# Two heads of a class side by side on the array, one accumulator, and attention work moved between the chunks of the query/key/value projection

## The chip, the cores and the metric

The kernel runs on one core of one Trainium2 chip. The metric is the device time of one execution in microseconds (us), and the median of several executions is what counts. Everything is 32-bit; weights and activations of the large products are split into a high and a low part, so that one product is three matrix multiplications.

## The reference

One inference step of a two-layer decoder trunk, for a prompt of 512 tokens and 8 sample tokens that share the weights: layer 0 is a gated short convolution, layer 1 a dilated sliding-window attention, and each is followed by a gated ConvFFN. The change is in layer 1:

```python
GROUPS = ((128, 1), (512, 4), (2048, 16))        # window, dilation; 8 heads of 64 in each group
q, k = rmsnorm(p[..., 0]), rmsnorm(p[..., 1])    # per head, p = h @ w_qkv
logits = einsum('bqhd,bqkhd->bqhk', q, kg) * SCALE + bias     # kg: the keys at dilated distances
out, lse = softmax(logits) @ vg, m + log(s)
w = softmax(stack(lses)); out = sum(w[g] * outs[g])           # merge of the three groups
mp = op @ attn_w_out                                          # and the same for the sample tokens, with caches
```

## The kernel before

The five engines run programs written out by hand, one block each (`block.sync`, `block.scalar`, `block.vector`, `block.tensor`, `block.gpsimd`), and meet at semaphores. The order of the code is the order of the work. All weights pass through the same pipeline of **chunks** of 1024 x 128 weights: SP loads a chunk into one of four slots (`load`), ScalarE copies its high part (`split_hi`, L711), VectorE subtracts for the low part (`split_lo`, L1016), and TensorE multiplies (`products`, L1508). A chunk is 8 k-steps of 6 matmuls each with 260 columns, 48 in all. Its result lands in one of two accumulators `acc[:, 0]` and `acc[:, 1]`, taken in turn (`cc % 2`).

The attention layer is the stage `S_QKV` of 36 chunks: four passes p = 0 to 3, one for each pair of heads, with nine chunks c = 0 to 8 (query, key, value of three groups). VectorE reads each result (`tile_out`), ScalarE squares it, TensorE sums over a head (`head_sums`, L1711), ScalarE makes the inverse root (`head_rms`), VectorE multiplies (`normalise`, L1306), and keys and values are transposed (`kv_transpose`).

The attention of pair p-1 runs among the chunks of pass p. Queries fall into four classes (position mod 4), and the softmax of one head and one class is a **unit**; a pair of heads has eight. All three groups are merged in a single softmax over 768 logits. A unit is: `unit_logits` (L1679 with 512 columns, L1680 and L1681 with 128, contraction over the 64 rows of one head), `unit_softmax` on VectorE (L1246, L1250, then L1256, L1257) around `exp_unit` on ScalarE (L876), `unit_transpose` (L1497, six of them), copies out of PSUM (`pt_copy` L882 on ScalarE, `unit_pt` L1230 on VectorE), `unit_values` (L1699, L1700, L1703) and `unit_o` (L1238). TensorE does all of that at one place, before k-step 3 of a chunk: `products(..., {3: at})`. Once in a pass, at c = 8, `sample_values` (L1778) multiplies the cached values of the eight sample tokens: 24 products of two columns, in one run.

After chunk 35 the last pair's attention runs among the eight small chunks (three k-steps, 18 matmuls) of the output projection `S_WO` (`part_products`, `part_residual`). Then come the last k-step of that projection (L1883) and the second ConvFFN. I call the stretch from the end of chunk 35 to L1883 the **stage end**.

In the trace, 32-bit matmuls of attention appear as two instructions (two **passes**); L1508 and transposes appear as one.

Of the kernel before, what the change touches and what calls it, by code (L numbers as in the profile page):

```python
# [143 lines left out]
def build(nc, x_prompt, x_sample, state_sc, cache1, cache4, cache16, state_ffn, norm_mix, norm_ffn, sc_w_in,  # L144
# [10 lines left out]
    with ExitStack() as ctx:  # L155
# [32 lines left out]
        small = sb("small", [P, 8])  # L188
# [23 lines left out]
        inv = attn(2 * TT).rearrange("p (t n) -> p t n", t=2)  # L212
        v_t = attn(2 * SEQ).rearrange("p (t n) -> p t n", t=2)
# [3 lines left out]
        lg = attn(6 * P)  # L217
        pr = attn(6 * P)
# [62 lines left out]
        softmax_steps = sem("softmax_steps")  # L281
        neg_ready = sem("neg_ready")
        e_ready = sem("e_ready")
        p_ready = sem("p_ready")
        pt_ready = sem("pt_ready")
        pt_act = sem("pt_act")
        pt_dve = sem("pt_dve")
        o_ready = sem("o_ready")
        o_kept = sem("o_kept")
        kt_ready = sem("kt_ready")  # L290
        vt_ready = sem("vt_ready")
        kt_kept = sem("kt_kept")
        vt_kept = sem("vt_kept")
# [71 lines left out]
        PT = (lg[:, 0:4 * P], lg[:, 4 * P:6 * P])  # L365
        PT_LAST = (held[:, 0:4 * P], held[:, 4 * P:6 * P])
# [8 lines left out]
        def logit_parts(bank):  # L375
            return (bank[0:W, 0, HALF:HALF + P], bank[0:W, 1, HALF:HALF + P], bank[0:W, 1, HALF + P:HALF + P + SK[2]])
# [29 lines left out]
        def _(sp):  # L406
# [102 lines left out]
            def pair_rows_out(p):  # L509

                sp.wait_ge(vt_kept, 3 * p + 3)
                sp.wait_ge(kt_kept, 3 * p + 3)
# [19 lines left out]
            def sample_loads(ps, c):  # L532

                if c == 0:
                    if ps:
                        sp.wait_ge(samp_v, ps)
                    cache_rows(ps, 0, 0, skv[:, 0], skv_in[0])
                    sp.wait_ge(rowq_out, 16 * (ps + 1))
                    query_rows(ps, 0, skv[:, 1], skv_in[1])
                    cache_rows(ps, 1, 0, skv[:, 2], skv_in[2])  # L540
                    rows_to_dram(ps)
                elif c == 1:
                    pair_rows_out(ps)
                    sp.wait_ge(samp_prod, 3 * ps + 1)
                    query_rows(ps, 1, skv[:, 1], skv_in[1])
                elif c == 2:
# [3 lines left out]
                    fresh_rows(ps, 0, skv[:, 0], skv_in[0])  # L550
                    sp.wait_ge(samp_prod, 3 * ps + 2)
                    query_rows(ps, 2, skv[:, 1], skv_in[1])
                elif c == 3:
# [4 lines left out]
                elif c == 4:  # L558
# [6 lines left out]
            for cc in range(9 * NP_):  # L565
# [11 lines left out]
                if c == 8:  # L577
# [7 lines left out]
                    query_rows_to_dram(p)  # L585
# [5 lines left out]
            cache_rows(ps, 0, 0, skey(ps, 0), skv_in[0])  # L591
            sp.wait_ge(rowq_out, 16 * (ps + 1))
            query_rows(ps, 0, squery(ps, 0), skv_in[1])
            cache_rows(ps, 1, 0, skey(ps, 1), skv_in[2])
# [102 lines left out]
        def _(act):  # L697
# [241 lines left out]
            for cc in range(9 * NP_):  # L939
# [9 lines left out]
                if p and c < 8:  # L949
                    exp_unit(n0 + c)  # L950
# [998 lines left out]
```

## Time and profile before

| | us |
|---|---|
| median of 3 runs | 1432.86 (1432.2 to 1434.42) |
| the profiled execution, its own time | 1435.17 |
| its span, first to last instruction | 1433.5 |
| TensorE matmul busy | 1398.5 (98%) |
| VectorE busy | 766.1 (53%) |
| ScalarE busy | 506.3 (35%) |
| mean granted TensorE clock | 0.982 |

### The profile page before, as it was taken

How to read it: one execution, taken by the hardware profiler on the slowest of the kernel's cores; microseconds unless marked ns; L12 is line 12 of the kernel's file. 1: busy time of each engine (PE TensorE's matmuls, PEld its weight loads, DVE VectorE, ACT ScalarE, POOL GpSimd, SP SyncE). 2: the span in 40 equal slices, each digit the busy share in tenths (PEclk: the TensorE clock that was granted, in tenths of full speed). 3: DMA queues.
4: the chain of work that ended last, by engine and by line, in shares of the span. 5: the costliest groups of instructions: out<-in, count | busy, mean ns of one | idle time of the engine just before them, and what ended most of it. 6: DMA issues, size and time to landing. Idle time of an engine off the chain costs nothing.

```text
span 1433.5 us, 27779 instructions
## 1 busy us (share of the span) xinstructions
PE 1398.5 (98%) x11153; PEld 1353.7 (94%) x11153; DVE 766.1 (53%) x1250; ACT 506.3 (35%) x811; POOL 21.1 (1%) x50
## 2 busy tenths in 40 slices
PE   6999999999999999999999999989899999999998
PEld 5999999999999999999899899887799999999998
DVE  4655566556555433445655646647576565553222
ACT  4322234343333332334334333423353344332112
POOL 0000000000000000000000000000000000000000
PEclk9999999999999999999999999988799999999999
DMA  6354435654444444547526317337224454455331
GB/s 169 89 167 134 142 111 190 188 162 121 148 136 147 140 134 132 161 124 217 151 68 204 109 63 209 95 99 207 89 74 128 139 172 117 127 157 165 109 89 64
DMA packets 256586, 195.17 MB, mean 136 GB/s; under 512 B 6581, under 2 KB 250789, under 8 KB 255362
## 3 DMA queue, kind: packets, MB, share of 16 engines
q1 hardware_dynamic: 253528, 139.17, 34.3%
q0 software_dynamic: 1792, 54.43, 10.7%
q8 instruction: 53, 0.87, 0.3%
q10 hardware_dynamic: 1194, 0.54, 0.1%
q14 instruction: 19, 0.16, 0.0%
HBM read 186.60 MB, written 65.21 MB: 176 GB/s over the span
## 4 chain that ended last, share of the span: by engine, by line
PE 93%; DVE 3%; issue 1%; DMA 1%; ACT 1%; SPq 0%; DVEq 0%
PE acc L1508 78%; PE N L1497 3%; PE M L1679 2%; PE acc L1536 2%; PE acc L1778 2%; PE N L1711 2%; PE M L1703 1%; PE M L1699 1%; DMA wraw<-in_sc_w_in_dram 1%; PE M L1681 0%; PE M L1680 0%; DMA skv<-new_rows 0%; PE M L1536 0%; PE M L1700 0%; DVE wl L1016 0%
## 5 line engine op out<-in xcount | busy, mean ns | idle before, releaser
L1508 PE MATMUL acc<-hh,wh 128*128 128x260 f32 x2288 | 468.8, 286 | 0.9 <-DVE wl L1016 0.9
L1508 PE MATMUL acc<-hh,wl 128*128 128x260 f32 x2288 | 463.1, 284 | 0.0
L1508 PE MATMUL acc<-hl,wh 128*128 128x260 f32 x2288 | 462.7, 284 | 0.0
L711 ACT ACTIVATE wh<-wraw 128x1024 fp32r<-128x1024 f32 (+1 forms) x212 | 220.7, 1041 | 551.1 <-PE acc L1508 539.3
L1508 PEld LDWEIGHTS acc<-hh,wh 128*128 128x128 f32 x2288 | 356.7, 190 | 3.0 <-issue 1.1
L1508 PEld LDWEIGHTS acc<-hh,wl 128*128 128x128 f32 x2288 | 355.2, 190 | 0.0
L1508 PEld LDWEIGHTS acc<-hl,wh 128*128 128x128 f32 x2288 | 354.7, 190 | 0.0
L1016 DVE TENSOR_TENSOR wl<-wraw,wh 128x1024 fp32r<-128x1024 f32 (+1 forms) x212 | 254.3, 1199 | 176.7 <-ACT wh L711 171.1
L1508 PE MATMUL acc<-yh,wh 128*128 128x260 f32 x848 | 173.1, 285 | 0.0
L1508 PE MATMUL acc<-yh,wl 128*128 128x260 f32 x848 | 171.5, 284 | 0.0
L1508 PE MATMUL acc<-yl,wh 128*128 128x260 f32 x848 | 171.4, 284 | 0.0
L1508 PEld LDWEIGHTS acc<-yh,wh 128*128 128x128 f32 x848 | 131.4, 189 | 0.9 <-issue 0.4
L1508 PEld LDWEIGHTS acc<-yl,wh 128*128 128x128 f32 x848 | 132.0, 190 | 0.0
L1508 PEld LDWEIGHTS acc<-yh,wl 128*128 128x128 f32 x848 | 131.6, 190 | 0.0
L1180 DVE TENSOR_TENSOR u<-acc,r 128x512 f32<-128x512 f32 x44 | 30.4, 692 | 120.3 <-PE acc L1508 119.1
L876 ACT ACTIVATE big<-big,small 128x768 f32<-128x768 f32 x32 | 30.1, 939 | 106.9 <-DVE small L1250 106.9
L1497 PE MATMUL N<-ident,big 128*128 128x128 f32 (+4 forms) x307 | 43.2, 279 | 12.7 <-DVE big L1257 7.6
L810 ACT ACTIVATE sv<-cv 128x536 f32<-128x536 f32 x44 | 28.7, 652 | 73.6 <-DVE cv L1059 73.6
L1050 DVE TENSOR_TENSOR x<-acc,x 128x520 f32<-128x520 f32 (+1 forms) x24 | 16.8, 700 | 64.6 <-PE acc L1508 61.9
L1497 PEld LDWEIGHTS N<-ident,big 128*128 128x128 f32 (+4 forms) x307 | 35.4, 146 | 14.3 <-issue 12.7
L1188 DVE TENSOR_TENSOR t<-sv,r 128x512 f32<-128x512 f32 x44 | 30.5, 692 | 31.6 <-ACT sv L810 31.6
L1057 DVE SCALAR_TENSOR_TENSOR cv<-u,params,cv 128x536 f32<-128x536 f32 x52 | 40.4, 777 | 11.2 <-ACT cv L750 7.5
(205 smaller groups left out, 1194.9 us busy)
## 6 DMA issues: line engine op xcount, KB each, us to landing
out_dram<-in_cache_kv_d_dram POOLq DMA_DIRECT2D x24, 1364.0 KB, 6.3
wraw<-in_ffn_w_gate_dram SPq DMA_DIRECT2D x44, 512.0 KB, 3.8
wraw<-in_ffn_w_up_dram SPq DMA_DIRECT2D x44, 512.0 KB, 3.9
wraw<-in_attn_w_qkv_dram SPq DMA_DIRECT2D x36, 512.0 KB, 3.9
out_dram<-in_cache_kv_d_dram POOLq DMA_DIRECT2D x8, 2044.0 KB, 8.3
wraw<-in_ffn_w_down_dram SPq DMA_DIRECT2D x32, 448.0 KB, 3.7
wraw<-in_sc_w_in_dram SPq DMA_DIRECT2D x24, 512.0 KB, 3.9
wraw<-in_ffn_w_down_dram SPq DMA_DIRECT2D x16, 512.0 KB, 4.0
```

The source lines that it names most:

```text
L711: nc.scalar.activation(wh[c % 2][:, 0:k], wraw[:, c % 4, 0:k], ACT.Copy).then_inc(hi_done, 1)
L810: nc.scalar.activation(sv[:], cv[:], ACT.Silu).then_inc(silu_ready, 1)
L876: nc.scalar.activation(pr[:], lg[:], ACT.Exp, bias=small[:, 1:2], scale=-1.0, accum_out=small[:, 2:3]).then_inc(e_ready, 1)
L1016: V.tensor_tensor(wl[c % 2][:, 0:k], wraw[:, c % 4, 0:k], wh[c % 2][:, 0:k].bitcast(F32), ALU.subtract).then_inc(split_done, 1)
L1057: ch.after(V.scalar_tensor_tensor(out=cv[:], in0=u[:, 1:1 + CO], scalar=params[:, bass.ds(f + w1, 1)], in1=cv[:], op0=ALU.mult, op1=ALU.add))
L1180: V.tensor_tensor(u_prompt, acc[:, 0, :, 0:HP], prompt(r), ALU.mult)
L1188: V.tensor_tensor(prompt(t1), conv_prompt(sv), prompt(r), ALU.mult)
L1497: return T.transpose(out, in_, ident[0:k, 0:k])
L1508: ins = T.matmul(acc[:, par, h2, 0:HALF], w[c % 2][:, k, :], a[:, k0 + k, h2, :], start=(first and k == 0 and n == 0), stop=(last and k == ...
L1536: ins = T.matmul(dst[:, h2, 0:HALF], w[c % 2][:, k, :], a[:, k, h2, :], start=(first and n == 0), stop=(last and n == 2))
L1679: T.matmul(M[:, 0, :], k[s, 0, cq], k[s, 1, :], start=True, stop=True)
L1711: ins = T.matmul(N[:, h2, 0:HALF], head_ones[:], sq[:, h2, :], start=True, stop=True)
```

## The change

- **Units.** Both heads of a class are one unit now: four units a pair, 16 in all instead of 32. `unit_logits` takes head 0 on array rows 0 to 63 and head 1 on rows 64 to 127 in turn, with their results in separate PSUM banks; `unit_values` takes them on array columns 0 to 63 and 64 to 127 in turn. The number of matmuls per head is as before.
- **Places.** TensorE does nothing of the prompt's attention inside a chunk. Before an odd chunk c = 1, 3, 5, 7 stand the logits of a unit, with the values of the unit before between their two parts; before an even chunk 2, 4, 6, 8 stand its twelve transposes. `head_sums` and `kv_transpose` come one chunk later than before.
- **One accumulator.** From chunk 9 on all results go to `acc[:, 0]`, so a chunk may start only when `tile_out` has read the one before it. The banks `B0` and `B1` of `acc[:, 1]` hold logits, transposes and outputs of attention.
- **Softmax.** VectorE takes both heads' maxima in a row (`unit_max`), then scales head 0 (`unit_scale`); ScalarE scales head 1 (`scale_unit`) and makes all three copies after the transposes (`pt_copies`). `kv_transpose` results are copied by ScalarE alone.
- **Sample tokens.** `sample_values` is cut into eight pieces of three products, before k-steps 4 to 7 of chunk 8 and 0 to 3 of the next chunk. In SP's queue the sample loads of a pass move by up to a chunk, and `query_rows_to_dram` stands behind the wait on `samp_v`.
- **Stage end.** Four units with two small chunks each; all small chunks use `acc[:, 0]`.

```diff
+        def par(cc):
+            return cc % 2 if cc < 9 else 0
-        PT = (lg[:, 0:4 * P], lg[:, 4 * P:6 * P])
+        B0, B1 = acc[:, 1, 0], acc[:, 1, 1]
+        OUT = slice(2 * P, 3 * P)
...
             def unit_logits(n, between=None):
+                k, cls = qka[:, (n // NCLS) % 2], n % NCLS
+                heads = (slice(0, DH), slice(DH, P))
                 if n:
-                    pe.wait_ge(neg_ready, n)
-                T.matmul(M[:, 0, :], k[s, 0, cq], k[s, 1, :], start=True, stop=True)
-                T.matmul(M[:, 1, 0:P], k[s, 2, cq], k[s, 3, cq], start=True, stop=True)
-                T.matmul(M[:, 1, P:2 * P], k[s, 4, cq], k[s, 5, cq], start=True, stop=True).then_inc(s_ready, 1)
+                    pe.wait_ge(pt_kept, 3 * n)
+                for h2, s in enumerate(heads):
+                    ins = T.matmul(M[:, h2, :], k[s, 0, cq], k[s, 1, :], start=True, stop=True)
+                ins.then_inc(s_ready, 1)
+                if between:
+                    between()
+                for i in (1, 2):
+                    for h2, s in enumerate(heads):
+                        ins = T.matmul((B0, B1)[h2][:, (i - 1) * P:i * P], k[s, 2 * i, cq], k[s, 2 * i + 1, cq],
+                                       start=True, stop=True)
+                ins.then_inc(s_ready, 1)
...
             def unit_values(n, bank):
+                for i in (1, 2):
+                    for h2, s in enumerate(heads):
+                        T.matmul(bank[s, OUT], v[:, i, cls, s], pt_g12[:, (2 * h2 + i - 1) * P:(2 * h2 + i) * P],
+                                 start=(i == 1), stop=False)
                 for t in range(4):
                     lo, hi = 32 * t, min(32 * t + 64, P)
+                    for h2, s in enumerate(heads):
+                        ins = T.matmul(bank[s, OUT][:, lo:hi], v[:, 0, t, s], pt_g0[h2][:, t * P + lo:t * P + hi],
+                                       start=False, stop=(t == 3))
...
+            def pt_copies(n, bank):                          # ScalarE
+                act.wait_ge(pt_ready, 2 * n + 1)
+                nc.scalar.activation(pt_g0[0], bank[:, 0, :], ACT.Copy).then_inc(pt_kept, 1)
+                act.wait_ge(pt_ready, 2 * n + 2)
+                nc.scalar.activation(pt_g12, B1, ACT.Copy).then_inc(pt_kept, 1)
+                nc.scalar.activation(pt_g0[1], bank[:, 1, :], ACT.Copy).then_inc(pt_kept, 1)
...
-                products(S_QKV, 0, cc, cc % 2, DK, hh, hl, 0, True, True, first_chunk(2) if cc == 0 else {3: at})
+                elif p and c == 8:
+                    inserts = {k: (lambda b=k - 4, ps=p - 1: sample_values(ps, B0, b, b + 1)) for k in range(4, 8)}
+                elif p >= 2 and c == 0:
+                    inserts = {k: (lambda b=k + 4, ps=p - 2: sample_values(ps, B0, b, b + 1)) for k in range(4)}
+                free_acc(S_QKV, 0, cc, 2 if cc < 9 else 1)
+                products(S_QKV, 0, cc, par(cc), DK, hh, hl, 0, True, True, inserts)
...
+            for j in range(NCLS):                            # VectorE, stage end
+                unit_max(n, 0)
+                unit_max(n, 1)
+                if j == 3:
+                    sample_norm(p)
+                part_residual(2 * j)
+                unit_scale(n)
+                unit_inv(n)
+                splits(S_WO, 0, 2 * j)
...
+                part_residual(2 * j + 1)
+                splits(S_WO, 0, 2 * j + 1)
+                if j < 3:
+                    key_products(p, j)
+                    key_sums(p, j)
+                if j == 2:
+                    sample_max(p, N[:, 0])
```

On TensorE, in a pass p > 0 of the kernel before, this stands in the middle of a chunk between its third and fourth k-step: transposes of one unit, logits of the next, values of the first, head sums.

```order
L1508 MATMUL acc<-hh,wl 128x260 x2
L1497 MATMUL N<-ident,big 128x128 [waits p_ready,inv_ready]
L1497 MATMUL N<-ident,big 128x128 x5
L1679 MATMUL M<-big 128x512 [waits neg_ready]
L1680 MATMUL M<-big 128x128
L1681 MATMUL M<-big 128x128
L1699 MATMUL M<-big 64x128 [waits pt_dve,pt_act,o_kept]
L1700 MATMUL M<-big 64x128
L1703 MATMUL M<-big 64x64 x3
L1703 MATMUL M<-big 64x32
L1711 MATMUL N<-sv,head_ones 128x260 [waits qsq_ready]
```

In the kernel after, the same engine between an even chunk and the odd one behind it (L1701 and L1709 are the two parts of the logits of both heads, L1736 and L1741 the values of the unit before, L1749 the head sums; `newh_tok` and `big` hold the copied transposes):

```order
L1529 MATMUL acc<-hh,wl 128x260 x2
L1701 MATMUL M<-big 128x512 [waits pt_kept]
L1701 MATMUL M<-big 128x512
L1736 MATMUL acc<-newh_tok,big 64x128 [waits pt_kept]
L1736 MATMUL acc<-newh_tok,big 64x128 x3
L1741 MATMUL acc<-big 64x64 x6
L1741 MATMUL acc<-big 64x32 x2
L1709 MATMUL acc<-big 128x128 x4
L1749 MATMUL N<-sv,head_ones 128x260 [waits qsq_ready,inv_ready]
L1749 MATMUL N<-sv,head_ones 128x260
L1529 MATMUL acc<-hh,wh 128x260 [waits split_done,acc_free]
```

What was four changes of operation for one head is four for two heads now, the two heads alternate in each row, and the wait for the accumulator stands behind all of it.

On TensorE in chunk 8 of a pass, after the change, the sample tokens' values stand between k-steps, three products at a time (L1813):

```order
L1529 MATMUL acc<-hh,wl 128x260 x2
L1813 MATMUL acc<-cv,skv 128x2 x3
L1529 MATMUL acc<-hh,wh 128x260 x2
L1529 MATMUL acc<-hl,wh 128x260 x2
L1529 MATMUL acc<-hh,wl 128x260 x2
L1813 MATMUL acc<-cv,skv 128x2 x3
```

Before, L1778 stood there once with all 24 products in one row.

On VectorE, before the change, one unit stands in one chunk, and the reading of the chunk's result behind it (L1246 and L1250 the maxima, L1256 and L1257 the scaling, L1271 and L1273 the result's reading, L1016 the split):

```order
L1246 ISA big,small<-M,big 128x512 [waits s_ready]
L1246 ISA small 128x1
L1250 ISA big,small<-M,big,small 128x256 [waits dve_chain]
L1250 ISA small 128x1
L1356 RECIPROCAL small<-small 16x1 [waits samp_e]
L1357 TENSOR_SCALAR cv<-cv,small 16x323 [waits dve_chain]
L1256 RECIPROCAL small<-small 128x1 [waits e_ready]
L1257 TENSOR_SCALAR big<-big,small 128x768 [waits dve_chain]
```

After it, in an odd chunk, both heads' maxima stand in a row (L1252, L1256), then the split (L1030), `unit_o` (L1245) and the scaling of head 0 (L1263, L1264); the reading of the last chunk's result (L1283, L1285) stands ahead of them:

```order
L1252 ISA big,small<-M,big 128x512 [waits dve_chain,s_ready]
L1252 ISA small 128x1
L1256 ISA big,small<-acc,big,small 128x256 [waits s_ready,dve_chain]
L1256 ISA small 128x1
L1252 ISA big,small<-M,big 128x512 [waits s_ready]
L1252 ISA small 128x1
L1256 ISA big,small<-acc,big,small 128x256 [waits s_ready,dve_chain]
L1256 ISA small 128x1
L1030 TENSOR_TENSOR wl<-wraw,wh 128x1024 [waits hi_done]
L1245 COPY t<-acc 128x128 [waits o_ready]
L1263 RECIPROCAL small<-small 128x1 [waits e_ready]
L1264 TENSOR_SCALAR big<-big,small 128x768 [waits dve_chain]
```

The reading of the result moved ahead of the softmax, and the scaling of head 1 is no longer VectorE's.

## Rows read from the trace of the kernel before

**Rows 1.** The page: busy time, and the chain's shares by engine.

```profile
PE 1398.5 (98%) x11153; PEld 1353.7 (94%) x11153; DVE 766.1 (53%) x1250; ACT 506.3 (35%) x811; POOL 21.1 (1%) x50
PE 93%; DVE 3%; issue 1%; DMA 1%; ACT 1%; SPq 0%; DVEq 0%
```

**Rows 2.** Windows of passes 1 and 3 and the stage end: busy us, clock.

```profile
core 0: us, PE busy (x) PEld busy (x) DVE busy (x) ACT busy (x) POOL busy (x), PEclk, DMA share, GB/s
662.13:760.78 98.65, 97.92 (x744) 88.78 (x743) 57.57 (x124) 37.09 (x61) 0.49 (x1) 0.97 0.45 134
...
859.39:958.04 98.65, 97.92 (x744) 88.79 (x742) 56.73 (x124) 36.01 (x61) 0.99 (x2) 0.97 0.41 121
955.85:1030.95 75.10, 64.14 (x415) 54.50 (x413) 44.32 (x102) 21.86 (x41) 0.98 (x2) 0.84 0.61 174
```

**Rows 3.** TensorE's timeline, one insertion of pass 1: start us, us.

```profile
710.51 0.82 PE L1497 MATMUL N<-ident,big 128*128 128x128 f32 x6
711.26 1.12 PE L1679 MATMUL M<-big 64*128 64x512 f32 x2
712.22 0.38 PE L1680 MATMUL M<-big 64*128 64x128 f32 x2
712.44 0.38 PE L1681 MATMUL M<-big 64*128 64x128 f32 x2
712.75 0.43 PE L1699 MATMUL M<-big 128*64 128x128 f32 x2
713.02 0.38 PE L1700 MATMUL M<-big 128*64 128x128 f32 x2
713.25 0.60 PE L1703 MATMUL M<-big 128*64 128x64 f32 x8
713.77 1.14 PE L1711 MATMUL N<-sv,head_ones 128*128 128x260 f32 x4
```

**Rows 4.** Timeline of TensorE's weight loads, an insertion ten us earlier.

```profile
702.33 0.30 PEld L1681 LDWEIGHTS M<-big 64*128 64x128 f32 x2
...
703.14 0.59 PEld L1703 LDWEIGHTS M<-big 128*64 128x64 f32 x8
```

**Rows 5.** TensorE's timeline at c = 8 of pass 1.

```profile
744.45 0.40 PE L1699 MATMUL M<-big 128*64 128x128 f32 x2 [0.73 <-ACT big L882]
...
746.54 6.61 PE L1778 MATMUL acc<-cv,skv 128*128 128x2 f32 x48
```

**Rows 6.** Windows of L1778 alone (two), then of L1508 alone (two).

```profile
746.54:750.44 3.90, 3.90 (x36) 3.90 (x36) 1.00 0.50 196
750.44:753.01 2.57, 2.57 (x14) 2.57 (x13) 0.51 0.00 0
...
753.01:757.30 4.29, 4.29 (x20) 4.29 (x21) 0.50 0.01 4
757.30:760.78 3.48, 3.48 (x30) 3.43 (x29) 0.99 0.00 0
```

**Rows 7.** TensorE's waits from 958 to 1031 us: total, times, longest.

```profile
PE N L1497 <- DVE big L1257: 7.6, 6, 4.3
PE acc L1778 <- DVE cv L1364: 2.5, 1, 2.5
```

**Rows 8.** Timelines of VectorE and ScalarE, one chunk of pass 1.

```profile
704.11 0.67 DVE L1246 CUSTOM_DVE_ANT_0 big<-M,big 128x512 f32<-128x512 f32 x1
704.98 0.49 DVE L1250 CUSTOM_DVE_ANT_0 big<-M,big,small 128x256 f32<-128x256 f32 x1 [0.19 <-DVE small L1246]
...
706.77 0.62 DVE L1257 TENSOR_SCALAR big<-big,small 128x768 f32<-128x768 f32 x1
...
709.93 1.22 DVE L1016 TENSOR_TENSOR wl<-wraw,wh 128x1024 fp32r<-128x1024 f32 x1 [0.25 <-DVE big L1273]
...
705.51 0.94 ACT L876 ACTIVATE big<-big,small 128x768 f32<-128x768 f32 x1 [3.55 <-DVE small L1250]
```

**Rows 9.** SP's timeline in pass 2, and DMA issues from 660 to 860 us (KB each, us to landing).

```profile
770.08 6.35 SPq L515 DMA_DIRECT2D out_dram<-big  x1
...
skv<-in_cache_kv_d_dram SPq DMA_DIRECT2D x8, 512.0 KB, 5.5
```

More of the change, by code:

```diff
@@ new lines, in _ @@
+                if c in SUMS and p >= SUMS[c][0]:
+                    head_rms(6 * (p - SUMS[c][0]) + SUMS[c][1])
+                if c % 3:
+                    squares(6 * p + 2 * (c // 3) + c % 3 - 1)
+                if p >= 2 and c == 0:
+                    pair_y(p - 2)
+                    sample_y(p - 2, B0)
+            p, n0 = NP_ - 1, (NP_ - 1) * NCLS
+            step(S_QKV, 0, 9 * NP_ - 1)
+            head_rms(6 * NP_ - 1)
+            keep_queries(p, M[:, 0])
+            pair_y(p - 1)
@@ new lines, in _ @@
+                if p >= 2 and c == 0:
+                    unit_o((p - 1) * NCLS - 1, B1)
+                    pair_y(p - 2)
+                if c in SUMS and p >= SUMS[c][0]:
+                    normalise(p - SUMS[c][0], SUMS[c][1])
+                if p and c == 1:
+                    key_products(p - 1, 0)
+                if p and c == 2:
+                    key_sums(p - 1, 0)
+                    key_products(p - 1, 1)
+                if p and c == 4:
+                    key_sums(p - 1, 1)
+                    key_products(p - 1, 2)
+                    key_sums(p - 1, 2)
@@ L1419, in part_residual @@
+                if p and c == 6:
+                    sample_max(p - 1, B0)
+                if p and c == 7:
+                    sample_norm(p - 1)
+                if p and c == 8:
+                    sample_pts(p - 1, B0)
+                if p >= 2 and c == 0:
+                    sample_y(p - 2, B0)
             def part_residual(m):
@@ L1747, in sample_logits @@
                 pe.wait_ge(samp_lt, 3 * ps + 3)
-                for g, part in enumerate(logit_parts(bank)):
+                for g in range(NG):
+                    part = bank[0:W, SCOL[g]:SCOL[g] + SK[g]]
                     n = NBACK[g] + (1 if g == 2 else 0)
@@ L1818, in _ @@
-                free_acc(S_QKV, 0, cc)
+                n = (p - 1) * NCLS + (c - 1) // 2
+                if c in ROWS and p >= ROWS[c][0]:
+                    n_read(p, c)
+                    kv_transpose(p - ROWS[c][0], ROWS[c][1])
+                if p and c % 2:
+                    if c == 1 and p >= 2:
+                        pe.wait_ge(ys_lo, p - 1)
+                    if c == 1:
+                        pe.wait_ge(tb_in, 16 * p)
+                        pe.wait_ge(rowq_kept, p)
+                    if c == 7:
+                        pe.wait_ge(samp_m, p)
+                    if c == 1:
+                        unit_logits(n, lambda p=p: row_transpose(p - 1))
+                    else:
+                        unit_logits(n, lambda n=n: unit_values(n - 1, B1))
@@ L1868, in _ @@
-            sample_values(p, acc[:, 1], 4, 6)
-            unit_values(n0 + 7, N, PT_LAST)
-            sample_values(p, acc[:, 1], 6, NS)
+            part_products(1)
+            pe.wait_ge(kv_kept, 3 * NP_)
+            for j in range(NCLS):
+                if j == 3:
+                    pe.wait_ge(samp_m, NP_)
+                unit_transpose(n0 + j, N)
+                if j < 3:
+                    unit_logits(n0 + j + 1)
+                    part_products(2 * j + 2)
+                    unit_values(n0 + j, N[:, 1])
+                    if j == 2:
+                        sample_logits(p, N[:, 0])
+                    part_products(2 * j + 3)
```

493 lines of the change are left out of this document (206 added, 287 removed).

## The prediction

> **What bounds the kernel now.** First the page: TensorE is busy for 98% of the span and is 93% of the chain that ended last, while VectorE is busy for 53% [rows 1]. So a saving on TensorE is a saving of time, and one on VectorE is not. The questions are what TensorE does in the attention layer, and where it waits or runs slowly. The windows answer both [rows 2]: the passes 1 to 3 (three of them, first and last shown) take 98.65 us each with TensorE busy for 97.9, VectorE for 57. The stage end takes 75.10 with TensorE busy for 64.1, so it is a chain of waits there. The granted clock is 0.97 in a pass and 0.84 in the stage end.
>
> The timeline of one insertion [rows 3] gives the price of a head's unit: transposes 710.51 to 711.26, 0.75; logits to 712.75, 1.49; values to 713.77, 1.02. That is 3.26 us for each of 32 units, none of it waiting. The timeline at c = 8 shows a stall of 0.73 before the values and then the sample tokens' run of 48 passes, 746.54 to 753.01, 6.47 us [rows 5]. The windows of that run alone [rows 6] say more: 36 passes in 3.90 us at a clock of 1.00, so 0.108 each, then 0.51, the 1.2 GHz level; and the 20 matmuls of the chunk behind it took 0.215 each at 0.50, where 30 took 0.116 each at 0.99. TensorE fell to the low level in the middle of a run of two-column products and stayed there for some 6.8 us.
>
> **What the change saves on TensorE.** (a) *Sample values between k-steps.* 48 passes by 0.108 are 5.2 against 6.47: 1.27. The 20 slow matmuls cost 20 x (0.215 - 0.116) = 1.98. Both passes shown have the same clock and length, so I take three such places: 9.7. In 24 pieces there is an edge each; I allow 0.05 for one, 1.2. Left: 8.5. It assumes that the clock stays at 1.00 when half of the time between pieces is 260-column work (three products, 0.65, then a k-step, 0.7).
>
> (b) *The 0.73 stall* [rows 5]: the values waited for ScalarE's copy right behind the transposes. After the change a chunk lies between. Three times: 2.2.
>
> (c) *Fewer changes of operation.* Six transposes take 0.75 where five spacings of 0.108 and a pass would be 0.65; L1681 holds TensorE for 0.31 before L1699, where L1680 took 0.22 [rows 3]. So a change of shape costs about 0.1. Before there are four a head, eight a class, after it five a class: 0.3 by 16 classes, 4.8. Matmuls and columns are otherwise the same. The Trainium skill (TensorEngine Tiling, Key Properties) says that a change of tiling mode drains the engine, which speaks against putting the values between the two parts of the logits; the trace has the drain at about 0.1 us, and by it the count of changes still falls.
>
> (d) *Two heads on two halves.* The trace of before has no two matmuls on different halves next to each other, so I bound it. Each product is two passes, and the second of a head must follow its first. In the row head 0, 0, head 1, 1 only neighbours of different heads can run together: four 512-column passes take three slots, eight 128-column passes five. Lowest: nothing, 0. Highest: logits' first part, one slot of 0.48 (0.96 for two passes, L1679); second part, three of 0.11, 0.33; values' 128-column passes, 0.33; the short ones, 0.53 a head for eight, seven of 16 slots of 0.066, 0.46 [rows 3]. That is 1.60 a class, 25.6 in all. Between them: the weight loads. Two loads of 128 columns of weights come 0.11 apart, (0.30 less one load of 0.19), and eight of 64 columns 0.065 apart [rows 4], which is as long as the passes that they feed. If loads go on one after another, then the second part of the logits and the short values gain nothing, the 512-column passes gain their 0.48 and the values' 128-column passes (loads of 64 columns) 0.33: 0.81 a class, 13.0 us. I take this one: it is in the middle, and the rows show TensorE's short passes spaced as their loads are.
>
> **What it costs.** (e) *One accumulator.* `free_acc` now waits for the read of the chunk just ended: 0.68 and 0.15 on VectorE and a hand-over, about 1.1 after the last matmul. Between chunks TensorE has at least 12 transposes and head sums, 1.3 + 0.8; that hides it. Only before chunk 9 there are head sums alone and VectorE reads a value tile: 0.7 once. (f) *The softmax of two heads in one chunk.* Counted from the end of the logits: maxima of two heads 2.0 (0.49 + 0.67 + 0.49 and the gaps of 0.2 between) [rows 8], split 1.2, `unit_o` 0.4, reciprocal and scaling 0.8, the other reciprocal 0.2, ScalarE's scaling 0.9: 5.5. The chunk takes 5.8 and head 0's transposes 0.65 more. It fits by 0.9, so 0. VectorE's 57 us per pass [rows 2] fit too in some 90. (g) *SP's queue.* The cache and query loads now wait for sample products in the middle of the next pass's first chunk, some 5 us into it, and the small query rows go out behind a 512 KB load that takes 5.5 to land; SP itself is held for 6.35 by one row-out DMA [rows 9]. Queued behind the waiting SP are the second query broadcast and the weights; the weights have four chunks to spare. VectorE's `key_products` of c = 2 I reckon late by 2 to 4 us, and behind it stand the next `tile_out` and maxima; TensorE's 4 us of work before chunk 3 cover most. I allow 1 a pass, 3.
>
> (h) *Stage end.* Before: waits of 7.6 and 2.5 for VectorE [rows 7] and 0.9 before L1883. After, in order: TensorE waits for `ys_lo`, since ScalarE copies the 1024 columns of `kv_transpose` before `sample_y`, about 2.0; the second small chunk waits for the first one's `part_residual`, which stands behind four maxima, 0.9; each `unit_logits` now follows its transposes directly and waits for ScalarE's three copies, 3 x 1.4; and at j = 2, `sample_max` waits for `sample_logits`, and behind it on VectorE stand both maxima, `sample_norm` and `part_residual(6)`, for which the seventh small chunk waits: 1.2 + 2.8 + 0.6 + 0.8, about 5.5. Sum 12.6 against 11.0: a loss of 1.6. Its slow stretches (0.16 of 75.1, 12 us before) I leave as they are: the 4.3 us wait goes, a 5.5 us wait comes. The saving of (c) and (d) there is counted.
>
> Sum: 8.5 + 2.2 + 4.8 + 13.0 - 0.7 - 3.0 - 1.6 = 23.2. The profiled execution took 1435.17, so 1412.0; it lies 2.3 above the median 1432.86, and against that the forecast is **1409.6**.
>
> **The rivals.** *No overlap at all.* The halves run one after another: 13.0 less, 1422.6. For it: passes before were never closer than their own length. Against it: they always used the same rows. *Full overlap*: 12.6 more, 1397.0. For it: loads on different halves read different partitions, and nothing in the rows forbids two at once. The Trainium skill (TensorEngine Tiling, Key Properties) says so: different tiles can load weights and multiply in parallel; no row here shows two at once. *The clock falls all the same* in the cut-up sample values: half of their time is two-column work. Then (a) keeps nothing of 1.27 + 1.98 at three places, 9.7 back: 1419.3. For it: the fall came after 3.9 us of such work [rows 6]; against it: insertions of 3 to 4 us with fp32 work at full width never brought it [rows 2, 3]. *Slower than before*: the two-head softmax does not fit into a chunk, and TensorE waits before the transposes at twelve even chunks, with the clock falling where the wait is long. It decides from 23.2 / 12 = 1.9 us a place, so if the chain of (f) is 2.8 longer than reckoned; at 3 us a place the time is 1409.6 + 36 = 1446. VectorE at 57 of 98 us speaks against it, the key products in the same queue for it. *The change does nothing* on balance, because the stage end loses what the passes gain: it would need a stage end of 98 instead of 75 us; 1433.
>
> **How the numbers follow.** Likeliest case 0.48 (alone 1403 to 1417), no overlap 0.22, full overlap 0.13, clock falls 0.10, slower 0.05, nothing 0.02. The range for 8 in 10 runs from 1396 (full overlap) to 1424 (no overlap, and the clock case); what it leaves out is the slow rival, a combination of no overlap with a falling clock or longer waits, and a stage end without slow stretches on top of full overlap. A measurement of this kernel tells about 0.2%, 2.9 us, from no change. Faster by more than that: all cases but the last two and a part of no overlap with the clock falling, 0.92; same 0.03; slower 0.05.
>
> **What would show each step.** In the profile after: the windows of a pass near 90 us and the clock in it 1.00 (a); no stall of 0.7 at L1736 (b); starts of head 1's 512-column passes with or right behind head 0's second, and first parts of logits lasting 1.4 rather than 1.9 (d); TensorE's waits for `acc_free` and p_ready below 1 us a pass (e, f); VectorE's waits for DMA at `key_products` of a few us a pass (g); in the stage end one wait of about 5 us before the seventh small chunk, three of 1.4 before logits, and a stretch near 76 us (h). The prediction is wrong if 512-column passes of two heads stand 0.43 apart throughout, if the clock in c = 8 falls to 0.5, or if TensorE's waits in the three passes come to more than 10 us.

## The result and the profile after

The kernel after takes **1395.2 us** (median of 4, 1393.51 to 1396.47), against 1432.53 (median of 4) for the one before, measured together: ratio 0.9738, 95% interval 0.9721 to 0.9755. That is 37.3 us faster, where I forecast 23.2 (1409.6), and it lies 0.8 below the lower end of my range. The profiled execution took 1394.49, its span is 1392.9, the mean granted clock 0.989.

The page of the kernel after, TensorE and VectorE, and the chain by engine:

```profile
PE 1348.9 (97%) x11153; PEld 1312.0 (94%) x11153; DVE 727.9 (52%) x1170; ACT 528.3 (38%) x839; POOL 21.2 (2%) x50
...
PE 91%; DVE 2%; SPq 2%; DMA 2%; issue 1%; ACT 1%; DVEq 0%
```

TensorE has the same 11153 instructions as before [rows 1] and 49.6 us less busy time. The same work got shorter, and only in part because the clock was better. The windows of the kernel after (us, busy time, then clock) are pass 1, pass 2, the third from the same mark to the end of chunk 35, and the stage end:

```profile
661.28:749.81 88.53, 85.80 (x744) 78.08 (x742) 47.68 (x103) 42.39 (x68) 0.49 (x1) 1.00 0.50 148
749.81:843.02 93.21, 87.80 (x743) 80.53 (x742) 47.71 (x103) 42.60 (x68) 0.99 (x2) 0.96 0.48 143
843.02:922.30 79.28, 76.28 (x642) 69.36 (x641) 42.19 (x94) 38.88 (x61) 0.99 (x2) 0.98 0.44 136
922.30:989.53 67.23, 54.89 (x467) 47.58 (x466) 39.41 (x90) 29.62 (x54) 0.99 (x2) 0.87 0.65 195
```

A pass took 98.65 before [rows 2]. Pass 1 now takes 88.53 with the clock at 1.00, but pass 2 takes 93.21 with the same matmuls: something costs 4.7 us there that pass 1 has less of. The stage end went from 75.10 to 67.23, though more work lies in it now. The last head sums, the values of the last class of the pair before and half of its last sample values stand behind chunk 35 (922.30 to 927.01, 4.7 us), where before they stood inside it.

Where in the kernel the profiled pair differs, the next windows show. The first two are before and after, from the start of the attention layer's second chunk to the same product of the second ConvFFN. The last two, before and after, are a stretch of layer 0, whose code the change leaves alone:

```profile
605.02:1053.64 448.62, 432.29 (x3211) 392.86 (x3209) 260.71 (x548) 169.25 (x276) 4.43 (x9) 0.95 0.44 131
...
601.71:1012.23 410.52, 385.47 (x3211) 353.83 (x3209) 222.30 (x468) 191.21 (x304) 4.45 (x9) 0.96 0.47 143
...
180.24:187.63 7.39, 7.39 (x49) 7.39 (x49) 5.33 (x9) 1.25 (x2) 0.00 (x0) 0.77 0.54 154
...
178.46:184.34 5.88, 5.88 (x50) 5.88 (x49) 5.33 (x9) 1.26 (x2) 0.00 (x0) 1.00 0.68 189
```

So 38.1 us of the 40.7 between the two profiled executions lie in the attention layer. In e8, a second profile of the kernel after, the same stretch takes 410.66. The starts say that 3.3 (605.02 less 601.71) lie ahead of the layer. Of that, 1.8 comes before the first L1508, at 44.32 (the same product starts at 42.53 after, and anywhere from 42.45 to 44.42 in the other runs below), and 1.5 in the stretch of layer 0 shown, which ran in part at the low clock before and not after (in e7 it took 7.39 again). Both are differences between executions, not the change. Behind the layer 0.8 is lost again, of which I don't know the cause.

TensorE's timeline of a class in pass 1, both heads (start us, us):

```profile
698.71 0.41 PE L1529 MATMUL acc<-hh,wl 128*128 128x260 f32 x2
699.05 1.13 PE L1701 MATMUL M<-big 64*128 64x512 f32 x4
700.11 0.66 PE L1736 MATMUL acc<-newh_tok,big 128*64 128x128 f32 x8
700.60 0.61 PE L1741 MATMUL acc<-big 128*64 128x64 f32 x16
701.13 0.71 PE L1709 MATMUL acc<-big 64*128 64x128 f32 x8
701.78 1.14 PE L1749 MATMUL N<-sv,head_ones 128*128 128x260 f32 x4
```

Read it by the starts: four 512-column passes in 1.06, eight 128-column passes of the values in 0.49, sixteen short ones in 0.53, eight 128-column passes of the logits in 0.65. That is 2.73 us for the logits and values of two heads, where two heads took 2 x (1.49 + 1.02) = 5.02 before [rows 3]. One 512-column product, two passes, was 0.96 there. Two of them now take 1.06, so each pass of one head runs beside a pass of the other. The same timeline, asked for only up to 699.1, holds two of the four already, which start within 0.01 us of each other:

```profile
699.05 0.70 PE L1701 MATMUL M<-big 64*128 64x512 f32 x2
```

The timeline of the weight loads at the same place shows the same of the loads. Sixteen of 64 columns take 0.60, less one load of 0.14, so they start 0.031 apart on average, where they were 0.065 apart before [rows 4]:

```profile
700.49 0.60 PEld L1741 LDWEIGHTS acc<-big 128*64 128x64 f32 x16
```

The Trainium skill (TensorEngine Tiling (Array Packing), Key Properties) says that different tiles load weights and multiply in parallel, and here the trace agrees, with the 1.06 and the 0.60 above. The Trainium skill (TensorE: Matmul & The Clock Gate, Part 3) lets loads overlap with running matmuls only where the row groups differ. The values of two heads lie on the same rows and on different columns, and their loads ran from 700.49 to 701.09 while their passes ran from 700.60 on, so for these column halves the trace does not bear that out.

The twelve transposes of a class stand in one row, and take 1.31 where they took 2 x 0.75 before [rows 3]:

```profile
708.54 0.60 PE L1518 MATMUL M<-ident,big 128*128 128x128 f32 x4
...
709.85 0.39 PE L1749 MATMUL N<-sv,head_ones 128*128 128x260 f32 x1
```

TensorE's waits from 600 to 1050 us (total, times, longest):

```profile
PE acc L1529 <- DVEq L1304: 10.3, 4, 5.4
PE acc L1529 <- DVE x L1440: 5.2, 2, 4.4
PE M L1701 <- ACT big L894: 3.5, 3, 1.2
PE M L1701 <- DVE yl L1382: 1.7, 1, 1.7
...
PE M L1813 <- DVE cv L1375: 1.0, 1, 1.0
PE M L1909 <- issue: 0.9, 1, 0.9
PE N L1518 <- ACT big L902: 0.9, 1, 0.9
```

The first row is the accumulator, and it was waited for before chunk 3 of each of the passes 1 to 3 (1.6, 5.4 and 3.0; the fourth, 0.24, is before chunk 9). Here are TensorE's and VectorE's timelines at the longest such wait, in pass 2, and SP's timeline ahead of it:

```profile
775.89 0.80 PE L1529 MATMUL acc<-hh,wh 128*128 128x260 f32 x2 [5.41 <-DVEq L1304]
...
773.88 1.23 DVE L1350 TENSOR_TENSOR skv<-skv 128x1024 f32<-128x1024 f32 x1 [8.96 <-DMA skv<-new_rows]
775.02 0.68 DVE L1295 TENSOR_TENSOR big<-acc,r 128x512 f32<-128x512 f32 x1
```

```profile
756.34 4.42 SPq L512 DMA_DIRECT2D out_dram<-big  x1
760.79 5.65 SPq L516 DMA_DIRECT2D out_dram<-big  x8
...
767.73 0.42 SPq L501 DMA_DIRECT2D skv<-new_rows  x1
```

`key_products` (L1350) stands ahead of the reading of the chunk's result (L1295) in VectorE's order. It waited 8.96 us for the second query broadcast (L501), and that one was issued only at 767.73, after nine row-out DMAs of `pair_rows_out` (L512, L516) had held SP for 10.1 us. The idle TensorE then fell to the lower clock. These are two windows, around the ends of the waits of 5.4 and 3.0 us:

```profile
774.60:781.40 6.80, 5.51 (x25) 5.51 (x26) 5.60 (x16) 2.90 (x6) 0.00 (x0) 0.50 0.09 26
866.70:870.10 3.40, 3.40 (x15) 3.40 (x16) 3.27 (x9) 1.97 (x4) 0.00 (x0) 0.50 0.00 0
```

A chunk product took 0.215 us at 0.50 and 0.116 at 0.99 [rows 6], so these 10.2 us cost some 5.1 on top of the waiting, a little less where the first of them is still idle.

The rest of the waits inside the three passes is 0.9 for L902 and 0.3 for L1322, both before chunk 4 of pass 1 and right behind its 1.6. That makes 11.2 us in the passes, over the 10 that I had named as a sign of being wrong.

Chunk 8 with the cut-up sample values kept its clock, as this window of 10.46 us with 1.00 shows, which holds four of the eight pieces:

```profile
738.38:748.84 10.46, 10.46 (x101) 10.07 (x101) 4.73 (x9) 3.41 (x7) 0.00 (x0) 1.00 0.30 84
```

### The profile page after: what moved, and what is told of

It reads as the page before. It is cut to its first block, busy times and chain, and to the rows that moved or that the text cites. A ratio compares the mean times of both kernels' runs of the same rounds, so it can differ in the third digit from the quotient of the medians.

```text
span 1392.9 us, 27664 instructions
## 1 busy us (share of the span) xinstructions
PE 1348.9 (97%) x11153; PEld 1312.0 (94%) x11153; DVE 727.9 (52%) x1170; ACT 528.3 (38%) x839; POOL 21.2 (2%) x50
## 4 chain that ended last, share of the span: by engine, by line
PE 91%; DVE 2%; SPq 2%; DMA 2%; issue 1%; ACT 1%; DVEq 0%
PE acc L1529 79%; PE acc L1557 2%; DMA skv<-new_rows 1%; PE N L1518 1%; PE N L1749 1%; SPq L516 1%; PE M L1701 1%; PE acc L1813 1%; PE M L1518 1%; PE acc L1518 1%; PE acc L1709 1%; DMA wraw<-in_sc_w_in_dram 1%; PE M L1813 1%; DVE wl L1030 1%; SPq L512 0%
## 5 line engine op out<-in xcount | busy, mean ns | idle before, releaser
L1529 PE MATMUL acc<-hh,wh 128*128 128x260 f32 x2288 | 468.6, 286 | 10.8 <-DVEq L1304 10.3
L1030 DVE TENSOR_TENSOR wl<-wraw,wh 128x1024 fp32r<-128x1024 f32 (+1 forms) x212 | 254.2, 1199 | 173.7 <-ACT wh L715 170.9
L1071 DVE SCALAR_TENSOR_TENSOR cv<-u,params,cv 128x536 f32<-128x536 f32 x52 | 40.4, 777 | 10.1 <-ACT cv L754 7.5
L1283 DVE TENSOR_TENSOR big<-acc,r 128x512 f32<-128x512 f32 x24 | 16.6, 691 | 52.7 <-PE acc L1529 52.7
L1073 DVE SCALAR_TENSOR_TENSOR cv<-u,params,cv 128x536 f32<-128x536 f32 x52 | 40.4, 777 | 6.5 <-DVE cv L1071 0.3
```

Source lines behind the costliest of these rows:

```text
L1030: V.tensor_tensor(wl[c % 2][:, 0:k], wraw[:, c % 4, 0:k], wh[c % 2][:, 0:k].bitcast(F32), ALU.subtract).then_inc(split_done, 1)
L1071: ch.after(V.scalar_tensor_tensor(out=cv[:], in0=u[:, 1:1 + CO], scalar=params[:, bass.ds(f + w1, 1)], in1=cv[:], op0=ALU.mult, op1=ALU.add))
L1073: V.scalar_tensor_tensor(out=cv[:], in0=u[:, 2:2 + CO], scalar=params[:, bass.ds(f + w2, 1)], in1=cv[:], op0=ALU.mult, op1=ALU.add).then_i ...
L1529: ins = T.matmul(acc[:, par, h2, 0:HALF], w[c % 2][:, k, :], a[:, k0 + k, h2, :], start=(first and k == 0 and n == 0), stop=(last and k == ...
```

## The experiments

All were timed beside the kernel before on the same chip, in three groups, in which the kernel before took 1432.07, 1433.42 and 1432.48. The kernel after, again in the second group (e8), took 1395.7.

### The two heads in turn (e1, e9)

The same matmuls in another order. In the values all of head 0's stand ahead of head 1's, as in this diff, and in the logits likewise (head 0's 512 columns; behind the values its 128-column products, then head 1's 512 and 128). VectorE is told of the first logits behind head 0's 512 columns alone.

```diff
-                for i in (1, 2):
-                    for h2, s in enumerate(heads):
-                        T.matmul(bank[s, OUT], v[:, i, cls, s], ...)
-                for t in range(4):
-                    for h2, s in enumerate(heads):
-                        T.matmul(...)
+                for h2, s in enumerate(heads):
+                    for i in (1, 2):
+                        T.matmul(bank[s, OUT], v[:, i, cls, s], ...)
+                    for t in range(4):
+                        T.matmul(...)
```

> The same matmuls as in the changed kernel, but head 0's first and head 1's behind them, in the logits and in the values, so that only one pair of neighbours in each part lies on different halves. Theory A (the saving of the halves comes from neighbours on different halves running at once, logits and values of a class 2.73 us instead of some 4.4): 1.7 us by 16 classes, about 1420 us. Rival B (the hardware brings the two heads together by itself, or the saving comes from fewer changes of operation): within 3 us of 1395.

Measured: 1416.2 (1413.74 to 1419.3), ratio 0.9892, 0.9872 to 0.9911. That is 21 us slower than the kernel after, and theory A's side. A class took 4.30 where it had 2.73, 25 us in sixteen, and the waits behind L1304 shrank from 10.3 to 1.8, because a later TensorE met VectorE ready. So the loss of overlap was partly paid for by waits that it hid. To see the price alone I repeated it on e7 (below), which has hardly any such wait in its passes.

> e7_loads_and_sample_order with the edit of e1_heads_in_turn: almost no waits are left in the passes that a later TensorE could hide, so the whole price of the lost overlap should show. Theory A (running the heads one after another costs 4.30 - 2.73 = 1.57 us for each of 16 classes, and e1 showed only 21 of these 25 because the waits for VectorE shrank from 10.3 to 1.8 us, with the low clock eating the difference of those): 25 over e7, 1397 to 1401. Theory B (part of e1's loss was the lower clock that happened to fall on it, and the overlap is worth 16 us or less): 1390 or less.

Measured: 1399.64 (1397.79 to 1400.9), ratio 0.9765, 0.9747 to 0.9782. The same kernel without the edit, again in this group (e11), took 1373.78, so the order of the heads alone is worth **25.9 us**. Theory A holds. The timeline of e9 at a class shows something more (L1702 and L1709 are the 512-column logits of head 0 and head 1, L1711 the 128-column ones of both, L1738 and L1742 the values):

```profile
701.11 1.12 PE L1702 MATMUL M<-big 64*128 64x512 f32 x2
702.16 0.65 PE L1738 MATMUL acc<-newh_tok,big 128*64 128x128 f32 x4
702.65 0.45 PE L1742 MATMUL acc<-big 128*64 128x64 f32 x5
702.88 0.32 PE L1738 MATMUL acc<-newh_tok,big 128*64 128x128 f32 x1
702.94 0.31 PE L1742 MATMUL acc<-big 128*64 128x64 f32 x3
703.04 0.49 PE L1738 MATMUL acc<-newh_tok,big 128*64 128x128 f32 x3
703.37 0.60 PE L1742 MATMUL acc<-big 128*64 128x64 f32 x8
703.90 0.37 PE L1711 MATMUL acc<-big 64*128 64x128 f32 x1
703.92 0.69 PE L1709 MATMUL M<-big 64*128 64x512 f32 x1
```

Head 0 has eight short passes (L1742), and head 1's first value pass started at 702.88 among them, ahead of three. The second head's 512-column pass started at 703.92, right beside the first of head 0's four 128-column passes at 703.90 and ahead of the other three, which stand before it in the program. So where the halves change, the next head's first pass starts while passes of the head before are still to come. Even "in turn" is not without overlap, and 25.9 is a lower bound on what the two halves are worth.

### The values alone in turn (e5)

The edit of e1 in `unit_values` only; the logits stay in pairs.

> The changed kernel, but in the values of a class all eight matmuls of head 0 are issued ahead of those of head 1; the logits stay in pairs. Theory A (matmuls overlap only where neighbours in the program's order lie on different halves, in the logits and in the values alike): the logits of a class stay at 1.70 us, the values go from 1.03 to about 1.9, 0.9 x 16 = 14 us more work of TensorE, less the waits for VectorE before chunk 3 that a later TensorE no longer meets (5 to 8 of the 10.3): 1402 to 1407. Theory B (only the long passes of the logits gain from neighbours; the short ones of the values overlap in any order): 1394 to 1397.

Measured: 1405.97 (1402.87 to 1409.38), ratio 0.9813, 0.9781 to 0.9844. The timeline of a class:

```profile
700.56 1.13 PE L1701 MATMUL M<-big 64*128 64x512 f32 x4
701.62 0.65 PE L1736 MATMUL acc<-newh_tok,big 128*64 128x128 f32 x4
...
703.37 0.71 PE L1709 MATMUL acc<-big 64*128 64x128 f32 x8
```

The 512-column passes still take 1.06, and the values went from 1.02 (700.11 to 701.13) to 1.75. That is 11.7 us in sixteen, less than the 14 that I wrote down, and the total, 10.3 over e8, is in theory A's range. The waits behind L1304 were 7.5 against 9.6 in e8. The passes of the values thus gain from neighbours as the long ones of the logits do. In my prediction the 64-column ones gained nothing. The edit moves the 128- and the 64-column passes together, and the two were not tried apart.

### The sample values in one run again (e2, e10)

```diff
-                    inserts = {k: (lambda b=k - 4, ps=p - 1: sample_values(ps, B0, b, b + 1)) for k in range(4, 8)}
-                elif p >= 2 and c == 0:
-                    inserts = {k: (lambda b=k + 4, ps=p - 2: sample_values(ps, B0, b, b + 1)) for k in range(4)}
+                    inserts = {4: (lambda ps=p - 1: sample_values(ps, B0, 0, NS))}
...
-            sample_values(p - 1, B0, 4, NS)
```

> The changed kernel with the 24 sample products in one run before k-step 4 of chunk 8, as before the change. Theory A (the clock falls in such a run: 1.3 us in the run and 2.0 in the chunk behind it, at three places): about 1405 us, with the granted clock at 0.5 behind each run. Rival B (the cut only matters for the edges; the run gives the samples' results earlier and so SP's loads too): 1393 to 1396.

Measured: 1402.71 (1399.9 to 1403.72), ratio 0.979, 0.9774 to 0.9807, so 7.5 over the kernel after's 1395.2. Again the waits behind L1304 were shorter (7.9), so I repeated it on e7:

> e7_loads_and_sample_order with the edit of e2_sample_run_whole: the same for the sample values. Theory A (a run of 48 two-column passes brings the lower clock by itself, 2 to 3.3 us at each of three chunks 8): 7 to 10 over e7, 1381 to 1384. Theory B (in e2 the clock fell because of waits in the neighbourhood): within 3 us of e7.

Measured: 1383.03 (1379.28 to 1383.23), ratio 0.9644, 0.9625 to 0.9663: **9.3 us** over e11, where I had forecast 8.5. Some 1 us of it is new waits of TensorE (0.6 for L1323, 0.2 for L903, 0.2 for L1383), so the run itself costs about 8.3. The windows of e10 at chunk 8 of pass 1, of which the first two are the run itself, show the clock falling inside the run and staying down for the first chunk products behind it:

```profile
731.02:735.00 3.98, 3.98 (x36) 3.98 (x34) 0.00 (x0) 0.00 (x0) 0.00 (x0) 0.91 0.54 210
735.00:738.19 3.19, 3.19 (x17) 3.19 (x17) 0.00 (x0) 0.00 (x0) 0.00 (x0) 0.50 0.00 0
738.19:741.25 3.06, 3.06 (x15) 3.06 (x16) 0.00 (x0) 0.00 (x0) 0.00 (x0) 0.53 0.00 0
```

TensorE was busy throughout and waited for nothing. It is the two-column work by itself that brings 1.2 GHz here, and full-width products in between keep 2.4 GHz. Theory A holds.

### The row-outs behind the query broadcasts (e3)

SP's queue alone: the nine row-out DMAs move from c = 1 to c = 5, and the second query's loads from c = 2 to c = 1.

```diff
                 elif c == 1:
-                    pair_rows_out(ps)
-                elif c == 2:
                     rows_to_dram(ps)
                     sp.wait_ge(samp_prod, 3 * ps + 1)
                     query_rows(ps, 1, skv[:, 1], skv_in[1])
+                elif c == 2:
...
+                elif c == 5:
+                    pair_rows_out(ps)
```

> The changed kernel with the nine row-out DMAs of a pair moved in SP's queue from c = 1 to c = 5, so that the second query broadcast goes out as soon as VectorE has used the first. Theory A (TensorE's 10.3 us of waits before chunk 3 come from that broadcast, late behind the row-outs in SP's queue): they go, and with them two slow stretches, about 1382 us. Rival B (the DMA engines are full there whatever the order): VectorE waits as long as before, 1391 to 1397.

Measured: 1381.3 (1379.5 to 1383.35), ratio 0.9643, 0.9627 to 0.9659: 14 us under the kernel after, with the same work on every engine. Theory A holds. The two moves, the row-outs later and the loads earlier, were not tried apart. No wait before chunk 3 is left, for the 0.2 below is the one before chunk 9. A new one came, 2.3 before chunk 2 of pass 2, since the first query broadcast is late there too:

```profile
PE acc L1530 <- DVEq L1288: 2.3, 1, 2.3
...
PE acc L1530 <- DVEq L1305: 0.2, 1, 0.2
```

### The sample maximum later (e4)

In the stage end, `sample_max` moves from j = 2 to behind `part_residual(6)`, and the rest of the sample's softmax behind the last unit's.

```diff
-                if j == 3:
-                    sample_norm(p)
                 part_residual(2 * j)
+                if j == 3:
+                    sample_max(p, N[:, 0])
...
-                if j == 2:
-                    sample_max(p, N[:, 0])
```

> The changed kernel with the sample tokens' maximum of the stage end moved on VectorE behind the residual of the seventh small chunk, and their exponential and scaling behind the last unit's. Theory A (the seventh small chunk waits 4.4 us because the residual stands behind the sample maximum): the wait goes, with the slow stretch of 3.4 us behind it, about 1390 us. Rival B (the wait moves to the last transposes or the last sample products): 1394 to 1397.

Measured: 1393.82 (1389.74 to 1395.4), ratio 0.9728, 0.9708 to 0.9749. Mostly theory B, 0.2 below its range: the 4.4 us wait before the seventh small chunk went, and another grew from 1.0 to 2.5 at the sample products at the end:

```profile
PE M L1813 <- DVE cv L1375: 2.5, 1, 2.5
```

The 1.4 us by which the medians differ is inside what this comparison can tell.

### The loads in order, and then the sample's softmax too (e6, e7, e8, e11)

e6 is e3, with the first query's rows written ahead of SP's wait for the sample values, and at the stage end `sample_y` ahead of `keep_kv` on ScalarE.

```diff
                 if c == 0:
+                    query_rows_to_dram(ps)
                     if ps:
                         sp.wait_ge(samp_v, ps)
                     cache_rows(ps, 0, 0, skv[:, 0], skv_in[0])
-                    query_rows_to_dram(ps)
...
             pair_y(p - 1)
-            keep_kv(p, 2)
             sample_y(p - 1, B0)
+            keep_kv(p, 2)
```

> As e3_row_outs_behind_queries, and the first query's rows go out ahead of the wait for the sample values' weights in SP's order, and ScalarE makes the sample products' input ahead of the kept kv of the pass. Theory A (what is left of the waits before chunks 2 and 3 is a place in SP's order, and each wait also costs a stretch at the lower clock): the 2.3 us wait of e3 and its 1.7 us at the lower clock go, and 0 to 1.7 at the stage end: 1376 to 1379. Theory B (VectorE's own work is what TensorE meets next): as e3, 1381 or more.

Measured: **1378.61** (1378.32 to 1379.13), ratio 0.9615, 0.9592 to 0.9638, in theory A's range. Neither chunk 2 nor chunk 3 waits any more, and VectorE's wait for `new_rows` fell from 20.9 to 0.5.

e7 is e6, with the sample's softmax spread out: the maximum as in e4, its exponentials ahead of `scale_unit`, its norm right behind `unit_inv`, its transposes' copies ahead of the last split.

> As e6_loads_in_order, and at the stage end the sample's softmax is spread out: its maximum behind the seventh small chunk's residual, its exponentials ahead of the last scaling, its norm right behind the last inverse. Theory A (the 4.4 us wait before the seventh small chunk is a turn in VectorE's order that can be given to others without loss): 3 to 5 us under e6, 1371 to 1375. Theory B (as e4: wait and lower clock only move to the sample products at the end): within 1.5 us of e6.

> The changed kernel unaltered, on the same chip as the other three: 1394 to 1396 by every theory; what it differs from that is what the chip adds to the others' times.

> e7_loads_and_sample_order unaltered, on the chip of the other two: 1373 to 1375 by every theory.

Measured: e7 **1373.81** (1373.59 to 1374.85), ratio 0.9582, 0.9559 to 0.9605; e11, the same, 1373.78 (ratio 0.959); e8 1395.7 (1394.54 to 1396.2; ratio 0.9735). So theory A for e7, 4.8 under e6. e4 had found the right wait but moved it into the next engine's way; with the exponentials and the norm brought forward as well it goes. TensorE's waits in e7 from 909 to 970 us, and the window of its stage end:

```profile
PE M L1702 <- ACT big L895: 3.5, 3, 1.2
PE N L1519 <- DVE t L1246: 0.9, 1, 0.9
...
PE acc L1530 <- DVE x L1441: 0.8, 1, 0.8
...
```

```profile
909.66:969.59 59.93, 53.26 (x467) 46.16 (x466) 39.34 (x90) 29.85 (x54) 0.98 (x2) 0.91 0.77 219
```

The stage end is 59.93 against 67.23 in the kernel after, with a clock of 0.91 for 0.87: less waiting, and less time at 0.50. e7 beats the kernel before by 59.6 us and the kernel after by 21.9, both measured beside it.

## Why the prediction was wrong

The direction, the order of events and most places were right. The range failed on one term.

**(d) Two heads on two halves: the step that failed.** It forecast 13.0, and in its bound "full overlap" 25.6. Two sentences carried it. "The second of a head must follow its first ... four 512-column passes take three slots" counted 0.48 saved on the first part of the logits. The profile shows two slots, first passes together and then second passes together: 1.92 became 1.06, 0.86 saved. Even my upper bound was too low, because I let the program's order (head 0, 0, head 1, 1) decide what may run together, while a free half goes on with the next product, in e9 even ahead of three passes that stand before it. And "loads go on one after another" gave the logits' second part and the short values nothing. They save 2 x 0.53 - 0.65 = 0.41 and 2 x 0.52 - 0.53 = 0.51; the values' 128-column passes save 2 x 0.50 - 0.49 = 0.51 (0.33 forecast). The four sum to 2.29 a class, where (c) and (d) had 0.3 + 0.81. The loads of both halves ran side by side. e5 shows this for the short passes, and e1 and e9 show that it hangs on neighbours in the order.

**(c) Fewer changes of operation.** Forecast 4.8, and not tried by itself. The transposes went from 2 x 0.75 to 1.31 (708.54 to 709.85), 0.19 a class. A row of twelve has 0.109 a transpose, so the six of before hold 0.10 for the change to the logits, and 0.19 is two such changes. In the kernel after the logits stand right behind a chunk, and the change moved there: from 698.71 the chunk's last two passes take 0.34 to the start of the logits, where two passes take 0.24, so 0.10 is lost again. I had counted four changes a head before and five a class after. At transposes to logits, logits to values and values to head sums it was three a head, and four a class are left, so (c) is worth about 2 x 0.1 x 16 = 3.2, an estimate. Both terms together: 16 x (2.29 + 0.19 - 0.10) = **38.1 against 17.8**, with 25.9 of it shown by e9 to be the order of the heads.

**(a) Sample values between k-steps.** Forecast 8.5, e10 measured 9.3, or 8.3 without its new waits. Right in mechanism and size: the clock stays at 1.00. The rival "the clock falls all the same" is excluded.

**(b) The stall.** Forecast 2.2. No wait stands before L1736 in the list, so it went.

**(e) One accumulator.** Forecast 0.7. Before chunk 9 the wait was 0.24 (at 655.41), and the transpose ahead of it fills 0.3 of the time. Elsewhere it costs nothing, as long as VectorE isn't held up by something else. That is what (g) did.

**(f) The softmax of two heads in a chunk.** Forecast 0. No wait of TensorE in passes 1 to 3 stands on the scaling of head 0, and one of 0.9 on ScalarE's scaling of head 1 (L902). That one is gone in e3, where only SP's order differs, so it belongs to (g). The slower rival had no case.

**(g) SP's queue: mis-sized.** The mechanism was named, but with 1 us a pass, 3 in all. It was 10.0 of waits before three chunks (the 0.24 before chunk 9 is (e)), 1.2 before chunk 4, and 5.1 for the low clock behind the long ones, 16.3 in this profile. e6 removed 17.1 against e8, of which 1.7 is the wait for `sample_y`, and **15.4** is left. I had seen the one row-out DMA of 6.35 us [rows 9], but not counted the eight behind it that stand ahead of the second query's rows in the same queue. "2 to 4 us late" became 9 on VectorE, and the 4 us of cover on TensorE left 5.4. I had also priced the wait without the clock.

**(h) Stage end.** Forecast 12.6 of waits for 11.0. The four named ones measured 1.7 (2.0), 0.8 (0.9), 3.5 (4.2) and 4.4 (5.5). With 1.0 and 0.9 at the end, which I had left out, that is 12.3, a loss of 1.3 for 1.6. The slow share, which I left as it was, went from 0.16 of 75.10 to 0.13 of 67.23, from 12.0 to 8.7, a gain of at most 3.3, since a slow stretch costs nothing where TensorE is idle. The stretch itself came to 67.23, not near 76, although 4.7 of other work moved into it.

**A term that I had left out.** Before the change TensorE waited 1.57 for ScalarE's squares at the first head sums of the layer, which stand inside a chunk. With the head sums a chunk later that wait is gone:

```profile
608.91 1.14 PE L1711 MATMUL N<-sv,head_ones 128*128 128x260 f32 x4 [1.57 <-ACT sv L964]
```

The sum with these: 38.1 + 8.3 + 2.2 - 0.2 - 15.4 - 1.3 + 3.3 + 1.6 = 36.6. The attention layer differs by 38.1 in the two profiled executions, and the medians differ by 37.3. So 0.7 to 1.5 us aren't placed, and the agreement is no closer than the terms, several of which are good to 1 us at best. Two errors had opposite signs, 20.3 too little for (c) and (d) and 12.4 too little cost for (g), so the prediction was closer than its terms by luck.

## What to carry to other kernels

Products that use only half of the array's rows or columns are worth pairing, head beside head, in the program's order. Here two cost hardly more than one, down to 64-column passes with a weight load each, and their order alone was worth 26 us. When an accumulator becomes single, its reader must not stand behind anything that waits for a DMA. Follow each such DMA back through its queue, and count every instruction ahead of it there. A long wait of TensorE costs more than itself: those of 5.4 and 3.0 us here had a stretch at 1.2 GHz behind them. The one of 1.6 had none, but the length of the wait alone doesn't decide: that of 1.7 in the stage end, which has sample products close ahead, had one (L1701 took 2.08 at 929.82, for 1.13 at 699.05). Moving one instruction may only move the wait (e4), so move the whole chain behind it (e7).

## What was unexpected of the hardware

- Two 32-bit products of 512 columns on different halves of the rows took 1.06 us, as against 0.96 for one. Sixteen 64-column passes on different halves of the columns took 0.53, as against 0.52 for eight. I had expected the two passes of one product to stay together.
- Passes on different halves did not start in the program's order. With heads in turn, head 1's first 512-column pass started at 703.92, ahead of three 128-column passes of head 0 that stand before it (from 704.12, e9).
- 48 two-column passes without a wait brought the clock to 0.50, in the kernel before and in e10; the same 48 in eight pieces between full-width products kept it at 1.00.
- What stays open: the last sample products (L1813, 6.15 us) ran at a granted clock of 0.50 from first to last, in the kernel after (983.38 to 989.53) and in e7 (963.44 to 969.59). Cutting these up too was not tried.
